# A hybrid decoder layer on one core: the copies and convolution taps of the delta stage, each moved by one place

## The reference

```python
qkv = silu(causal_depthwise_conv(concat([qd, kd, vd]), conv_w))       # 4 taps
qd, kd = l2norm(qd) * HEAD_DIM_K ** -0.5, l2norm(kd)
decay = exp(where(incl, gc[:, None] - gc[None, :], -inf))             # per chunk
a = where(strict, beta[:, None] * (k @ k.T) * decay, 0.0)
sol = triangular_solve(eye + a, concat([beta * v, beta * exp(gc) * k]))
u_bar, w = sol[..., :dv], sol[..., dv:]
qk = (q @ k.T) * decay
def step(state, xs):                                                  # over chunks
    u = u_bar_c - w_c @ state
    o = q_c @ state + qk_c @ u
    state = gl_c * state + k_c.T @ u
```

## Time and profile before

| what | value |
|---|---|
| median of three runs | 2422.68 us (2420.56 to 2422.92) |
| the profiled execution, its own time | 2422.92 us |
| its span, first to last instruction | 2421.2 us |
| TensorE busy | 2327.4 us, 96% of the span |
| VectorE, ScalarE, GpSimd busy | 913.3, 697.6 and 658.9 us |
| mean granted TensorE clock | 0.989 |
| time of one pass of the delta loop | 83.07 us |

### The profile page before, as it was taken

The page is one execution under the profiler, slowest core; times in us unless marked ns, Lnnn a source line. Parts: engine busy times, 40 slices in busy tenths (PEclk is TensorE's granted clock), DMA queues, the critical chain, the costliest instruction groups (busy, mean ns, idle before and its releaser), DMA issues.

```text
span 2421.2 us, 31268 instructions
## 1 busy us (share of the span) xinstructions
PE 2327.4 (96%) x11568; PEld 1926.7 (80%) x11568; DVE 913.3 (38%) x1118; ACT 697.6 (29%) x1220; POOL 658.9 (27%) x447
## 2 busy tenths in 40 slices
PE   5999999999799999999999999998999999999998
PEld 4787888877588888888887888886888888888886
DVE  4415343444855564565543113313222112211234
ACT  4323233233454554555452210013110011100112
POOL 6252232212111111111112233332333233323331
PEclk8999999999899999999999999999999999999999
DMA  5112121203110221122023443331111111111112
GB/s 118 43 42 90 44 95 43 87 26 96 44 53 26 69 61 35 43 63 67 25 71 123 146 133 104 110 87 44 52 52 44 52 44 52 43 52 44 52 39 83
DMA packets 219107, 157.28 MB, mean 65 GB/s; under 512 B 22744, under 2 KB 205208, under 8 KB 217520
## 3 DMA queue, kind: packets, MB, share of 16 engines
q1 hardware_dynamic: 206528, 106.05, 15.7%
q10 hardware_dynamic: 12528, 50.53, 6.0%
HBM read 137.49 MB, written 19.07 MB: 65 GB/s over the span
## 4 chain that ended last, share of the span: by engine, by line
PE 87%; DVE 5%; DVEq 3%; DMA 2%; ACT 1%; issue 1%; POOL 1%; SPq 0%; ACTq 0%; POOLq 0%
PE bank L198 65%; PE bank L988 5%; PE bank L1221 2%; PE bank L1204 2%; DVEq L765 1%; DMA stat_b<-scr_stat 1%; PE bank L1159 1%; PE bank L1211 1%; PE bank L602 1%; DVE joint L769 1%; PE bank L1258 1%; PE bank L1178 1%; PE bank L1253 1%; PE bank L1240 1%; PE bank L1234 1%
## 5 line engine op out<-in xcount | busy, mean ns | idle before, releaser
L198 PE MATMUL bank<-u_hi,w_hi 128*128 128x512 f32 x2176 | 907.3, 417 | 15.6 <-DVE u_lo L1677 7.2
L198 PE MATMUL bank<-u_hi,w_lo 128*128 128x512 f32 x2176 | 852.8, 392 | 0.0
L198 PE MATMUL bank<-u_lo,w_hi 128*128 128x512 f32 x2176 | 850.8, 391 | 0.0
L184 POOL CAST w_hi<-raw 128x1024 fp32r<-128x1024 f32 (+1 forms) x176 | 183.8, 1044 | 1680.8 <-PE bank L198 1432.8
L198 PEld LDWEIGHTS bank<-u_hi,w_hi 128*128 128x128 f32 x2176 | 411.5, 189 | 91.1 <-DVE u_lo L1677 8.8
L198 PEld LDWEIGHTS bank<-u_hi,w_lo 128*128 128x128 f32 x2176 | 409.6, 188 | 88.8
L198 PEld LDWEIGHTS bank<-u_lo,w_hi 128*128 128x128 f32 x2176 | 412.0, 189 | 69.8 <-issue 3.8
L186 POOL TENSOR_TENSOR w_lo<-raw,w_hi 128x1024 fp32r<-128x1024 f32 (+1 forms) x176 | 429.5, 2440 | 25.7 <-issue 0.7
L1791 DVE TENSOR_TENSOR tmp<-tmp,bank 128x512 f32<-128x512 f32 x44 | 30.2, 687 | 367.3 <-PE bank L198 367.3
L198 PE MATMUL bank<-v_hi,w_hi 128*128 128x512 f32 x352 | 137.3, 390 | 2.6 <-DVE tmp L1791 2.6
L198 PE MATMUL bank<-v_hi,w_lo 128*128 128x512 f32 x352 | 137.0, 389 | 0.0
(11 more groups left out here) (247 smaller groups left out, 2713.6 us busy)
## 6 DMA issues: line engine op xcount, KB each, us to landing
raw<-in_w_in SPq DMA_DIRECT2D x84, 512.0 KB, 3.9
stat_b<-scr_stat ACTq DMA_DIRECT2D x12, 1024.0 KB, 6.8
row<-scr_rows ACTq DMA_DIRECT2D x24, 512.0 KB, 5.0
raw<-in_w_gate SPq DMA_DIRECT2D x22, 512.0 KB, 3.8
raw<-in_w_up SPq DMA_DIRECT2D x22, 512.0 KB, 3.8
scr_gate<-tmp ACTq DMA_DIRECT2D x16, 512.0 KB, 2.9
tmp<-scr_gate ACTq DMA_DIRECT2D x16, 512.0 KB, 4.3
raw<-in_w_down SPq DMA_DIRECT2D x16, 512.0 KB, 3.9
```

What stands on the lines that cost most here:

```text
L184: nc.gpsimd.tensor_copy(hi[:, 0:kt, :], raw[slot][:, 0:kt, :])
L198: last = nc.tensor.matmul(bank[dst][:, :], wpart[slot][wp][:, k, :], rhs[ap][:, k, half * HALF:(half + 1) * HALF], start=k == 0 and (wp, a ...
```

## The change

The table is changed in three places and ScalarE's copies of `a_right` in two. The step `t00` goes from column 19 to 20 and `t01` from 20 to 21; the eight half-row taps of v start in column 48 instead of 49, and the SiLU of v goes from column 59 to 58. The level-1 `a_right` copy goes from step `qk1` to behind the second `inv` copy of `t01`; the copy for level l+1 goes from behind the `inv_t` copy of step `p` to behind the `half_pair` copies of step `y`, which puts it ahead of the `inv_t` copy.

```diff
-                    19: ["qk1", "t00"], 20: ["t01"], 41: ["tt0", "tt1"], 43: ["ub0", "ub1", "wt0", "wt1"],
+                    19: ["qk1"], 20: ["t00"], 21: ["t01"], 41: ["tt0", "tt1"], 43: ["ub0", "ub1", "wt0", "wt1"],
...
-            TAPS_AT[49 + n_] = (2, n_ // 2, HALVES[n_ % 2])
-        SILU_AT = {30: 0, 46: 1, 59: 2}
+            TAPS_AT[48 + n_] = (2, n_ // 2, HALVES[n_ % 2])
+        SILU_AT = {30: 0, 46: 1, 58: 2}
...
                 f(z_now[:, :], z_next[:, :], ACT.Copy).then_inc(dl["z"], 1)
-                act.wait_ge(dl["a"], two + 2)
-                f(by_block(a_right[:, :], 1), side_columns(neg_a[:, :], 1, 1), ACT.Copy).then_inc(dl["ar"], 1)
...
                 f(c4(inv, half), bank[X0 + half][:, :].rearrange("p (c t) -> p c t", t=P), ACT.Copy).then_inc(dl["t0c"], 1)
+                if half == 1:
+                    act.wait_ge(dl["a"], two + 2)
+                    f(by_block(a_right[:, :], 1), side_columns(neg_a[:, :], 1, 1), ACT.Copy).then_inc(dl["ar"], 1)
...
                 f(half_pair[64:P, :, 64:P], y_now[64:P, :, 64:P], ACT.Copy).then_inc(dl["yc"], 1)
-            elif step[0] == "p":
-                level = int(step[1])
-                act.wait_ge(dl["pr"], h * 6 + level)
-                f(inv_t[:, 0:HALF], bank[X0][:, :], ACT.Copy).then_inc(dl["prc"], 1)
                 if level < 6:
                     f(by_block(a_right[:, :], level + 1), side_columns(neg_a[:, :], level + 1, 1), ACT.Copy).then_inc(dl["ar"], 1)
+            elif step[0] == "p":
+                act.wait_ge(dl["pr"], h * 6 + int(step[1]))
+                f(inv_t[:, 0:HALF], bank[X0][:, :], ACT.Copy).then_inc(dl["prc"], 1)
```

## The result

The changed kernel takes 2451.77 us (median of 4 runs, 2450.89 to 2454.68), the kernel before, run beside it, 2422.13 (4 runs): the ratio is 1.0127, with an interval of 1.0114 to 1.0140. It is slower, as forecast, but by more: 1.0127 times the 2422.68 us of before is 2453.4, 1.4 us over the upper end of the range, and the forecast was 2447.8. The profiled execution took 2451.97 us, with a span of 2450.2 against 2421.2 before: 29.0 us longer.

The account below looks back on a forecast made before the run. TensorE, busy 96% of the span, was taken as the bound. Copies and transposes, 2.11 us a head over eight heads (16.9), plus taps (8.05) made 24.9 us on 2422.92: 2447.8 us, range 2444 to 2452, low end widened to 2438.

Parts of the forecast that it names:

- TensorE at the limit, every stall counts in full: Delta stage: TensorE has 82.48 us of work in a pass of 83.07, so each added stall reaches the end in full.
- `y` of level 1: Step `y` of level 1 ends 0.87 us later per head, behind the later `t01` and the moved `a_right` copy.
- `a_right` ahead of `inv_t`: ScalarE: the moved copy delays `inv_t` and the `d` group by 0.52 us in level 1, 0.18 in levels 2 to 5.
- The taps: Scan: first v tap held to the end of GpSimd's `w_lo`, `u_now` of chunk 2 late: 1.15 us, seven passes, 8.05.
- The rival price: Scan: the tap creeps beside `w_lo` at a fifth of its speed; stall 0.93 us a pass, 6.5 in all.
- The upper price: Scan: the tap needs its whole 0.47 us after GpSimd's end; 1.41 us a pass, 9.9 in all.
- The pass h = 0: Last v tap ahead of two subtractions, one of which may miss or meet `w_lo`: taken as 0, 2.3 us either side.
- the sign of being wrong: A `d` group starting 0.24 us behind its triple as before despite a later `inv_t`, or a moved tap of 0.47 us.
- Only the copies cost: Rival: the tap is not held or finds GpSimd done, so taps cost nothing; 2439.8 us, chance 0.12.
- Only the taps cost: Rival: waits ahead of `d` are for `half_pair` and TensorE's own work, so copies hide; 2431.0 us, chance 0.05.
- No time: Rival: copies and taps both hide in slack on TensorE's queue that the rows don't show; 2422.9 us, chance 0.03.
- Faster by way of the pass h = 0: Rival: a subtraction gets through before `w_lo` is issued, worth up to 2.3 us; 2420.6 us, chance 0.03.

Follow-up runs that it names:

- the copies alone: Kernel before, with only the `a_right` copies of levels 2 to 6 moved ahead of the `inv_t` copy: 2437.0 us, ratio 1.0056.
- the transposes alone: Kernel before, with only `t00` and `t01` moved one column later: 2424.3 us, ratio 1.0003.
- the flat read: Kernel before with `a_right` copies of levels 2 to 6 moved, these reading 512 columns in a row instead of blocks of columns: 2439.0 us, ratio 1.0061.
- `half_pair` over 128 partitions: Kernel before with `a_right` copies of levels 2 to 6 moved, both `half_pair` copies made over 128 partitions instead of 64: 2425.0 us, ratio 1.0007.
- `p` with `y`: Kernel before, with step `p` of each level put behind step `y` in the same column: 2410.7 us; with `a_right` copies of levels 2 to 6 moved too, 2431.4.
- with the taps out of GpSimd's way: Kernel with `p` beside `y`, plus the fourth k tap one column earlier and the v taps one later than before: 2405.6 us, ratio 0.9928.

## Why the prediction was right and wrong

*TensorE at the limit, every stall counts in full: right.* A pass is longer by 3.85 us, and the change without its taps and the taps alone add up to that within 0.01.

*`y` of level 1: right.* 0.87 us forecast, 0.81 measured, of which `t01` alone is 0.35 (0.30 forecast). The group ends 1.22 us after the end of `a_right` (829.08 to 830.30), where the rule for the sum had 1.27.

*`a_right` ahead of `inv_t`: right as a mechanism, wrong in size, and this is the step that failed.* The prediction put it as "the next instruction starts about 0.11 before such a copy ends". That was read from `conv_in` to `inv_t` and from `inv_t` to `a_right` in the earlier trace rows, where it holds, and carried over to a place behind two copies of 64 partitions, where it does not hold. In all 40 such places of the changed kernel the next instruction starts 0.65 to 0.67 us after the start of `a_right`. Level 1 cost 0.66 instead of 0.52, levels 2 to 5 0.32 each instead of 0.18; with `y`, 0.81 + 0.66 + 4 x 0.32 = 2.75 a head instead of 2.11, and eight heads 22.0 instead of 16.9. The earlier trace rows could have warned: the `half_pair` row has no overlap worked into it (the sum starts `a_right` at 831.53, after the end of `half_pair` at 831.51), and no row shows an SBUF copy behind such a one. No bound was put on the term, though the price of an operation in a new place is one that the trace of before does not show; the range had room for the taps and the pass h = 0, and for this term none.

*The taps: right, in place, mechanism and size.* 1.15 forecast, 1.09 measured alone. The rival price, 0.93 by sharing, fell with the run that cut `w_lo` in two. The upper price of 1.41 has `u_now` start where the tap ends, while the other two have it start 0.08 us sooner; done alike it is 1.33, or 9.3 us, and the range would end at 2451.4.

*The pass h = 0: right within its bounds*, -0.36 us of 2.3 either way. Even that is not to be told from nothing: TensorE starts on `kn` at 641.81 before and at 641.45 now, and in the runs in which nothing of this pass was changed (the copies alone, the transposes alone, the change without the taps, the flat read, `half_pair` over 128 partitions, and `p` with `y` with and without the copies) it starts anywhere from 640.37 to 642.83. What the prediction left out is what follows. Behind this wait (the first row, of the changed kernel, against 15.67 in the earlier trace rows) the clock stays low, and it did so for longer in this execution. These rows are, of the changed kernel, the wait and two stretches (columns as in the earlier trace rows):

```profile
PE bank L1173 <- DVE kn L1353: 17.4, 1, 17.4
...
645.40:646.40 1.00, 1.00 (x6) 1.00 (x6) 0.62 (x2) 0.00 (x0) 0.00 (x0) 0.50 0.00 0
646.40:647.40 1.00, 1.00 (x4) 0.78 (x3) 0.87 (x2) 0.00 (x0) 0.00 (x0) 0.55 0.00 0
```

and of the kernel before:

```profile
643.80:645.80 2.00, 2.00 (x10) 1.80 (x9) 1.16 (x3) 0.00 (x0) 0.00 (x0) 0.50 0.00 0
645.80:646.40 0.60, 0.60 (x6) 0.59 (x6) 0.58 (x2) 0.00 (x0) 0.00 (x0) 0.99 0.00 0
```

At 0.50 TensorE has its lower level, 1.2 GHz. The kernel before is at the full one from 645.8, about 4 us after its wait ended at 641.81; the changed one is still at the lower nearly to 647.4, 6 us after 641.45. That is about 1.0 us of the first loop pass's 4.9, of which 3.85 are the pass itself. The longer wait is not what did it: the clock was low for about 4.0 us after 15.67 us of waiting before, but for 5.6 after 15.7 with `half_pair` over 128 partitions, for 5.4 after 13.8 in the change without its taps, and for 3.3 after 13.8 with the copies alone. So this 1.0 us, like the 1.4 at line 1651, differs from one execution to the next, and no run ties it to the change.

*The signs.* "Issue" ahead of the level-1 `d` group is 0.84 us (0.7 forecast), the wait of levels 2 to 5 is 13.0 / 32 = 0.41 (0.26 forecast), and the pass is 86.93 (86.3 forecast), all three off mainly by the same 0.14 a place. The tap of 2.34 us and the wait for `u_now` came as forecast. The 0.24 us in the sign of being wrong is no start: in the earlier trace rows a `d` group starts 0.18 or 0.08 behind its triple, and 0.24 is what it takes longer.

*The sum*, for the profiled executions. 7 x 3.85 = 27.0 for the passes in the loop, 1.0 for the low clock, 3.0 for head 7's stretch (2.75 by the copies; it has no such tap), less 0.4 in the pass h = 0, is 30.6, and less the 1.6 behind head 7 it is 29.0. The forecast had 24.9. The copies made 8 x (2.75 - 2.11) = 5.1 of the difference, and the rest takes 1.0 off again. The medians, over which the clock's luck of a single execution has less say, are 29.6 apart.

*The rivals.* Only the copies cost, 85.2 us a pass: fell, since the taps alone cost 1.09 us a pass. Only the taps cost, 84.2: fell, since the copies alone cost 1.93. No time: fell with both. Faster by way of the pass h = 0: fell; that stretch gained 0.36 us, and all the rest cost 29.

What stays open is why a copy over 64 partitions takes the overlap from the `a_right` copy behind it as well. That one reads SBUF; `conv_in`, which reads a bank, keeps its overlap in the same place (0.49 for 0.60). Whether the source makes the difference no run has tested.

## What to carry to other kernels

Where the bounding engine has no idle time, look for the copies that it waits for, and put no other instruction between such a copy and the work that feeds it. What helps is to issue the work that feeds the copy earlier, as step `p` beside `y` did (2410.7 us, and 2405.6 with the taps out of GpSimd's way, against 2422.7), not to shuffle the copies. And when an instruction is moved, take its duration from a start-to-start distance behind the very neighbours that it will have, or give the term a bound with no overlap at all: 5 x 0.14 us a head was the main error of this prediction.

## What the runs showed of the hardware

- ScalarE's copies over 128 partitions and 512 columns let the next one start 0.1 us before their recorded end (0.60 against 0.49; 0.63 against 0.52). Those over 64 partitions don't (0.40 from start to start for 0.38; over 128 partitions 0.28), and the `a_right` copy from SBUF right behind them doesn't either (0.66 for 0.63), while a copy out of a bank there does (0.49 for 0.60). With both `half_pair` copies over all partitions a pass was 83.36 us and not 85.00.
- VectorE's tap beside GpSimd's `w_lo` is held for one instruction, and not for as long as GpSimd is busy: with the same work cut in two, the tap took 1.24 us instead of 2.34, at a price of 0.32 us of GpSimd (2.72 against 2.40).
- A TensorE group of 8 small matmuls that waits for its release took 1.13 us, and the same with its operands in time 0.89.
- After a wait of TensorE of 12.5 to 17.4 us its clock was at the lower level for 3.3 to 5.9 us more, in 14 traces, and the longer wait did not go with the longer time.
